# In each weight piece, the products with the weights' high half come first, and the wait for the low half moves to the last third

## The reference, cut to what matters

```python
hn = rmsnorm(h, norm_g[i])
u  = hn @ w_in[i]                       # 2048 x 5632
ya = silu(layernorm(conv31(a_val * sigmoid(a_glu)) + b)) * silu(a_z)
yb = window_attention(q, k, v, bias, sink) * silu(b_z)    # 16 heads, banded
h  = h + concat([ya, yb]) @ w_out[i]    # 2048 x 2048
e  = rmsnorm(p[i] @ w_pe[i], pe_g[i])   # 256 x 2048
h  = h + e * sigmoid(h @ w_pg[i])       # 2048 x 2048
```

## Time and profile before

| what | value |
|---|---|
| median of 3 runs | 2078.45 us (2077.09, 2078.45, 2085.46) |
| the profiled execution, its own time | 2075.6 us |
| its span, first to last instruction | 2073.8 us |
| TensorE busy | 1965.5 us (95%), 14752 matmuls |
| weight loads busy | 1828.8 us (88%) |
| VectorE busy | 1354.5 us (65%) |
| ScalarE busy | 899.4 us (43%) |
| DMA queue of the weights | 319.85 MB, 51.4% of 16 engines' span |
| granted share of TensorE's clock, mean | 0.975 |

### The profile page before, as it was taken

One profiled execution on the slowest core, in us unless ns is written; L12 is line 12 of the kernel. 1 busy time (PEld: TensorE's weight loads), 2 busy tenths in 40 slices (PEclk: granted clock), 3 DMA queues, 4 the chain that ended last, 5 costly groups with the idle time before them and its releaser, 6 DMA issues.

```text
span 2073.8 us, 38777 instructions
## 1 busy us (share of the span) xinstructions
PE 1965.5 (95%) x14752; PEld 1828.8 (88%) x14752; DVE 1354.5 (65%) x2044; ACT 899.4 (43%) x1268; POOL 41.0 (2%) x47
## 2 busy tenths in 40 slices
PE   5998998999899899989996999999999999999997
PEld 5998888999899888889995889797989998888797
DVE  6699885765659988666667445546464656554554
ACT  4432545534443243554443344444444434355442
POOL 0000000000000000000000001000010000000000
PEclk8999999999999999999997999999999999999999
DMA  5665434555556544356563547464554664443443
GB/s 179 183 183 158 149 116 124 182 183 182 160 166 193 163 146 118 110 163 194 180 186 105 161 136 208 132 194 148 169 166 152 182 185 146 136 135 115 123 142 112
DMA packets 181152, 324.76 MB, mean 157 GB/s; under 512 B 13618, under 2 KB 32258, under 8 KB 180736
## 3 DMA queue, kind: packets, MB, share of 16 engines
q1 hardware_dynamic: 177936, 319.85, 51.4%
q10 hardware_dynamic: 3056, 2.77, 0.5%
HBM read 319.38 MB, written 2.69 MB: 155 GB/s over the span
## 4 chain that ended last, share of the span: by engine, by line
PE 74%; DVE 11%; issue 7%; ACT 6%; DMA 1%; ACTq 0%; DVEq 0%; POOL 0%; SPq 0%
PE g L439 57%; PE g L448 5%; DVE cacc L996 3%; DVE w_lo L785 3%; ACT u L1316 2%; ACT w_hi L1307 2%; PE scores L511 2%; PE weights_t L529 2%; PE misc L546 2%; PE weights_t L511 2%; PE att_out L546 2%; DVE q L840 1%; DMA sinks<-in_swa_sinks_dram 1%; ACT L1316 1%; DMA stage<-in_w_pe_dram 1%
## 5 line engine op out<-in xcount | busy, mean ns | idle before, releaser
L785 DVE TENSOR_TENSOR w_lo<-stage,w_hi 128x1024 fp32r<-128x1024 f32 x577 | 710.5, 1238 | 577.8 <-ACT w_hi L1307 577.4
L1307 ACT CAST w_hi<-stage 128x1024 fp32r<-128x1024 f32 x577 | 599.2, 1046 | 836.5 <-PE g L439 674.4
L439 PE MATMUL g<-a_hi,w_hi 128*128 128x256 f32 x2368 | 686.8, 290 | 25.3 <-DVE a_lo L853 14.1
L439 PE MATMUL g<-a_hi,w_lo 128*128 128x256 f32 x2368 | 675.7, 285 | 0.0
L439 PE MATMUL g<-a_lo,w_hi 128*128 128x256 f32 x2368 | 675.4, 285 | 0.0
L439 PE MATMUL g<-b_hi,w_hi 128*128 128x256 f32 x1824 | 529.9, 291 | 6.5 <-issue 5.2
L439 PE MATMUL g<-b_hi,w_lo 128*128 128x256 f32 x1824 | 517.7, 284 | 0.0
L439 PE MATMUL g<-b_lo,w_hi 128*128 128x256 f32 x1824 | 517.3, 284 | 0.0
L439 PEld LDWEIGHTS g<-a_hi,w_hi 128*128 128x128 f32 x2368 | 460.0, 194 | 43.7 <-issue 29.3
L439 PEld LDWEIGHTS g<-a_hi,w_lo 128*128 128x128 f32 x2368 | 460.4, 194 | 0.2
L439 PEld LDWEIGHTS g<-a_lo,w_hi 128*128 128x128 f32 x2368 | 459.9, 194 | 0.0
(11 more groups left out here) (178 smaller groups left out, 1394.5 us busy)
## 6 DMA issues: line engine op xcount, KB each, us to landing
stage<-in_w_in_dram SPq DMA_DIRECT2D x176, 512.0 KB, 3.7
stage<-in_fox_w_in_dram SPq DMA_DIRECT2D x128, 512.0 KB, 3.7
stage<-in_swa_w_in_dram SPq DMA_DIRECT2D x72, 512.0 KB, 3.8
stage<-in_w_out_dram SPq DMA_DIRECT2D x64, 512.0 KB, 4.1
stage<-in_w_pg_dram SPq DMA_DIRECT2D x64, 512.0 KB, 4.3
stage<-in_fox_w_out_dram SPq DMA_DIRECT2D x32, 512.0 KB, 4.2
stage<-in_swa_w_out_dram SPq DMA_DIRECT2D x32, 512.0 KB, 3.8
cm<-rel_scratch SPq DMA_DIRECT2D x4, 1536.0 KB, 7.6
```

The source lines that it names most:

```text
L439: mm = pe.matmul(acc[:, j * S:(j + 1) * S], w[:, slot, c0 + j * P:c0 + (j + 1) * P], xx[:, k, :], start=st and m == 0 and j % 2 == 0, stop ...
L785: dve.tensor_tensor(w_lo[:, slot, :], stage[:, slot, :], w_hi[:, slot, :].bitcast(F32), ALU.subtract).then_inc(*t.inc("w_split"))
L1307: act.copy(w_hi[:, slot, :], stage[:, slot, :]).then_inc(*t.inc("w_rounded"))
```

## The change

In `gemm_piece` the loop over steps, tiles and terms is turned round. The piece first waits for `w_rounded` alone. Then come, for step 0, the four matmuls w_hi*x_hi and the four w_hi*x_lo; the first slot's work; the same eight matmuls of step 1; then the wait for `w_split`, the four w_lo*x_hi of step 0 and the four of step 1, with the signal `w_used` on the last; and the second slot's work. The number and kind of matmuls stay. Where the activation is stationary and 512 columns move, a term has two matmuls in place of four.

```diff
--- before.py
+++ after.py
@@ -426,35 +426,38 @@
 
                 slot = piece[0] % RING
                 piece[0] += 1
-                pe.wait_ge(*t.see("w_split"))
-                for n in range(PK):
-                    k = order * PK + n
-                    st, end = first and n == 0, last and n == PK - 1
-                    mm = None
-                    c0 = n * CH
-                    terms = ((w_hi, xh), (w_lo, xh), (w_hi, xl))
+
+                def product(n, w, xx, opens, ends):
+
+                    k, c0, mm = order * PK + n, n * CH, None
                     if kind in ("T", "KV"):
                         for j in range(CT if kind == "T" else 2):
-                            for m, (w, xx) in enumerate(terms):
-                                mm = pe.matmul(acc[:, j * S:(j + 1) * S], w[:, slot, c0 + j * P:c0 + (j + 1) * P],
-                                               xx[:, k, :], start=st and m == 0 and j % 2 == 0, stop=end and m == 2,
-                                               skip_group_check=True)
+                            mm = pe.matmul(acc[:, j * S:(j + 1) * S], w[:, slot, c0 + j * P:c0 + (j + 1) * P], xx[:, k, :],
+                                           start=opens and j % 2 == 0, stop=ends, skip_group_check=True)
                     if kind in ("N", "KV"):
                         width = CH if kind == "N" else S
                         for b in range(NB):
-                            for m, (w, xx) in enumerate(terms):
-                                at = b * CH if kind == "N" else CH + b * S
-                                col = c0 if kind == "N" else c0 + S
-                                mm = pe.matmul(acc[:, at:at + width], xx[:, k, b * P:(b + 1) * P],
-                                               w[:, slot, col:col + width],
-                                               start=st and m == 0 and (kind == "N" or b == 0), stop=end and m == 2,
-                                               skip_group_check=True)
-                    if n == PK - 1:
-                        mm.then_inc(*t.inc("w_used"))
+                            at = b * CH if kind == "N" else CH + b * S
+                            col = c0 if kind == "N" else c0 + S
+                            mm = pe.matmul(acc[:, at:at + width], xx[:, k, b * P:(b + 1) * P], w[:, slot, col:col + width],
+                                           start=opens and (kind == "N" or b == 0), stop=ends, skip_group_check=True)
+                    return mm
+
+                def between():
                     if slots:
-                        s = slots.pop(0)
-                        for step in s:
+                        for step in slots.pop(0):
                             step()
+
+                pe.wait_ge(*t.see("w_rounded"))
+                product(0, w_hi, xh, first, False)
+                product(0, w_hi, xl, False, False)
+                between()
+                product(1, w_hi, xh, False, False)
+                product(1, w_hi, xl, False, False)
+                pe.wait_ge(*t.see("w_split"))
+                product(0, w_lo, xh, False, False)
+                product(1, w_lo, xh, False, last).then_inc(*t.inc("w_used"))
+                between()
 
             def chunk(kind, x_, parity, work=None, ready=False, order=INORDER, wait_all=False, pieces=PIECES):
 
@@ -666,6 +669,7 @@
             chunk("T", B, 0, ready=True, wait_all=True, work={11: [stats], 14: [spread_rs]})
             slot = piece[0] % RING
             piece[0] += 1
+            t.skip("w_rounded")
             pe.wait_ge(*t.see("w_split"))
             pe.wait_ge(*t.again("ob_free"))
```

## The result

The changed kernel took 2088.19 us (median of 20 runs, 2085.52 to 2102.72), the kernel before 2078.87 us beside it (20 runs, 2077.09 to 2085.75). The ratio is 1.0053, 95% interval [1.0038, 1.0068]: half a per cent slower, where I had forecast 2082 us, a loss of 3.5 us, and a range of 2070 to 2088. The profiled execution took 2087.64 us (span 2085.7), against 2075.6 (span 2073.8) before, so the two traces to be compared lie 11.9 us apart. Of the 20 runs of the changed kernel, 13 lie at 2085.5 to 2089.2 us with a mean granted clock of 0.971 to 0.974, the profiled one among them, and 7 at 2096.3 to 2102.7 us with 0.964 to 0.966, by that clock some 25 us more at half rate, for a reason that stays open.

What follows compares the result with a forecast made beforehand. TensorE is busy nearly throughout, but VectorE sets the time from 89 to 189 us; afterwards waits alternate. Terms of +0.36 us a pass, twice +0.7, and +2.8 once make +3.5 on 2078.45, about 2082 us; range 2070 to 2088.

Steps and rivals of the forecast that it cites:

- The low half: Rival: the low half was the bound, so VectorE's chain shortens; -10.1 us, 2068 us; chance 0.07.
- the first score: Near 189 us: the wait for VectorE's `q` grows from 3.98 to about 5.9 us; worth 0.
- `stats`: First chunk, slot 8: work comes 0.48 us earlier and its 0.89 us wait grows; +0.48 us a pass.
- the first head: First transposed head, first attention, slot 6: waits longer for VectorE's normalisation, 1.05 for 0.57 us; +0.48 us a pass.
- `turn_lf`: Slot 4, once: work that waited 3.01 us comes earlier; +0.48 us.
- the fox heads: First transposed head in "fox", slot 6, four times: arrives just at the moment, 0.48 us each; +1.9 us.
- `ln_spread`: Last big chunk, slot 12: the 0.51 us wait goes and the slot comes earlier; -1.0 us a pass.
- Near 166 us: Wait for the low half stays, now mid-piece; TensorE leaves about 1.9 us ahead but then waits for `q`; worth 0.
- All others have room: Remaining slot work costs nothing; the nearest is the attention product, with 0.69 us, of which 0.21 stay.
- The clock: Behind the wait for `q`: longer idleness can start the half rate earlier; +0.3 us a pass, between -1.65 and +0.6.
- it does nothing: Rival: casts are no earlier than needed and the slots' shifts cancel; 2078.5 us; chance 0.08.
- The sum's direct terms: Over the whole kernel: the forecast's longer waits of TensorE, without the clock term; +2.9 us.

Runs made afterwards that it cites:

- s12_scores8: Changed kernel with the first slot after 12 matmuls, but after 8 in the pieces that compute scores: 2082.97 us, 1.0009 of the kernel before.
- s12_late: Changed kernel with only the first slot put back behind 12 matmuls, the late wait for the low half kept: 2076.76 us, 0.9998 of the kernel before.
- s12_early: Changed kernel with the low half waited for at the piece's start and the first slot behind 12 matmuls: 2078.07 us, 0.9997 of the kernel before.
- old_s8: Kernel before, old order and wait kept, with only the first slot moved from 12 to 8 matmuls: 2086.07 us, 1.0036 of the kernel before.
- s8_late_but_conv: Changed kernel with the low half waited for at the piece's start in pieces 32 to 49 of each pass: 2087.42 us, 1.0039 of the kernel before.
- s8_early: Changed kernel with the low half waited for at the start of every piece, first slot still behind 8: 2086.51 us, 1.0040 of the kernel before.

## Why the prediction was wrong, point by point

*Right.* The spacing holds; a window of the changed kernel answers to the earlier trace rows:

```profile
402.00:562.00 160.00, 159.06 (x1325) 158.80 (x1323) 100.16 (x95) 68.97 (x67) 1.30 (x2) 1.00 0.60 188
```

1325 matmuls in 159.06 us are 0.120 us each, with the second wait in every piece; no stream is broken. The low half was not the bound: its waits are gone and the one at the first score went from 3.98 to 6.35 us (forecast 5.9), so of the 3.5 us a pass that it waited near 145 and 166 us nothing is gained. The score starts 1.54 us later (forecast 0.5): 0.48 is the slot's at `stats`, 0.62 came with the start of the kernel and 0.37 from `spread_rs`, below. The waits at `stats` (1.34 us, forecast 1.4), the first head (1.05, forecast 1.05), `turn_lf` (3.01 to 3.49) and the fox heads (no wait before, 0.39 to 0.44 now, four times) each grew by about a slot shift of 0.48 us. At `ln_spread` the gain is there too, in another place than I wrote: the wait for `glu` behind it fell from 5.30 to 4.75 us and the 0.51 us for `w_lo` vanished, together 1.06 a pass, forecast 1.0. Waits for `pt` stayed under the 2 us of the forecast, at 1.1 (0.5 before).

*Near 166 us.* I expected a wait for the low half in the middle of the piece. It stands at the piece's head, 2.73 us, for the high half: the ScalarE cast is itself the late one there. That changes nothing in the sum, as VectorE sets the time up to the first score.

*"All others have room": the step that failed in kind.* For `spread_rs` of the first chunk I read no wait in the trace of before and took that for room. There is 0.21 us of waiting at 52.80 now, and it starts 6.67 us behind `stats` where it was 6.30 (51.81 against 45.51, a row below). Its input comes from VectorE behind a split, the split behind a cast, and that cast behind the end of a piece which `stats` has delayed. The trace has this chain: the cast went from 47.69 to 48.78 us, the split from 48.77 to 49.86. That is 0.37 us in the first pass; in the second no wait shows there. `turn_q` starts 0.24, 0.24 and 0.16 us behind the matmul ahead of it where it was 0.12, 0.3 us in all, and one attention product near 1967 us waits 0.63 us for ScalarE's `pt`. The row of before, in which TensorE arrives in the same moment:

```profile
51.81 0.60 PE L495 MATMUL misc<-diag,ones 128*128 128x256 f32 x2
```

An instruction that follows its neighbour without a gap tells that it waits for nothing now, not how long it may be early. Together the missed places are about 1.3 us of the 11.9.

*The clock: the term that was mis-sized.* The sum took +0.3 us a pass, with +0.6 as its upper bound: half of the 1.2 us by which the stretch could begin earlier. It did begin earlier, and lasted 10.2 us in place of 3.4 in the first pass (8.3 of work in place of 3.4) and 10.2 in place of 6.8 in the second (9.8 in place of 4.7); some 2.5 us a pass at this place, and 5.9 us of TensorE's busy time in all. I bounded how early the rate could fall and took for granted how long it would stay down, from a single stretch. The experiments showed in its place that the length does not follow the wait for `q`, which was what I had made the term hang on. It goes with the slot as far as one trace of each kernel tells: 10.2 us in all five with the slot at 8 throughout or nearly so and in s12_scores8, 6.8 in s12_late, s12_early and the three kernels with it at 16 or 20 throughout. What sets it is open. The Trainium skill ("TensorE: Matmul & The Clock Gate", Part 1: The HAM clock gate) has the engine fall to half rate when idle and be released by activity. As a rule that the trace can be held to: the release agrees, it always came with TensorE at work (at 193.3 us in s12_late, matmuls running since 188.68). What I drew from it, that one long wait is worse than scattered ones, is not borne out: the stretch behind 6.34 us of waiting in s12_late holds 4.7 us of work, the one behind 3.97 us in s12_early 5.4.

The rival "it does nothing" was right on the change's intent (s12_late, s12_early) and wrong on its side effect. The sum's direct terms, +2.9, and the missed places, 1.3, make 4.2 us of waits, against the 4.4 that are left of 6.0 without the 1.6 traded ahead of the first score; with the 5.9 us of slower matmuls and that 1.6 they make 11.7 of the 11.9 us between the profiled executions. Of the clock's share some 0.9 stand at the start of the kernel, before anything that the slot moves could matter: the half rate there ended at about 34.9 us instead of 33.1. These two rows, before and after, are windows from 33.1 to 35 us:

```profile
33.10:35.00 1.90, 1.90 (x18) 1.90 (x18) 0.31 (x1) 0.41 (x1) 0.00 (x0) 1.00 0.71 241
```

```profile
33.10:35.00 1.90, 1.90 (x11) 1.90 (x11) 0.04 (x1) 0.00 (x0) 0.00 (x0) 0.53 0.63 238
```

## What to carry to other kernels

When a piece of work is reordered, look first at where the work in between (the slots) ends up: here it was moved by 4 matmuls as a side effect, and old_s8 shows that this alone makes the loss. For each step in a slot ask how early it may come, from who produces its input, and not whether it waits today; and try the slot's place as a parameter of its own, since 8, 12, 16 and 20 matmuls gave 2088, 2077, 2075 and 2085 us. Where an engine is paced by its clock, bound how long a slow stretch can last as well as where it starts, and do not take its price from a single stretch: behind the same wait, stretches of 3.4 to 20.5 us stood in these traces.

## What the runs showed of the hardware

- A matmul stream with one more semaphore wait in each piece keeps 0.120 us from start to start (x1325 in 159.06 us).
- Behind the wait for `q` ahead of a pass's first score the stretch at 1.2 GHz lasted 3.4, 6.8 or 10.2 us, and once 20.5 (s12_scores8, second pass). The same group sequence behind the same kind of wait got the full rate back after 4.7 us in one kernel and 9.6 us in another.
- Behind waits of 3.97 or 3.98 us TensorE worked 3.4, 5.4 and 8.3 us at half rate (before, s12_early, s8_late_but_conv), behind one of 6.34 us 4.7 (s12_late), behind one of 4.43 us 9.8 (s8_early).
- Groups of four 64-row matmuls take 1.13 us at full and 2.07 us at half rate.
